# Hybrid encoder layer on one core: v quadrants and gate/up units loaded in the out projection pass, all w_out splits kept on chip, first down splits placed later

## The reference

```
u = _rmsnorm(h, norm1_g);  z = u @ w_in
a = gb * _short_conv(gc * xa, conv_w);  p = _multiscale_pool(xp, ...);  f = _fourier(xf)
mix = concatenate([_rms(a), _rms(p), _rms(f)]) * mix_g
h = h + mix @ w_out
v = _rmsnorm(h, norm2_g)
gu = v @ w_gate_up;  gate, up = gu[..., :D_FF], gu[..., D_FF:]
return h + (silu(gate) * up) @ w_down        # then a last RMSNorm
```

## Time and profile before

| what | value |
|---|---|
| median of 3 runs | 2538.41 us (2533.21 to 2539.73) |
| profiled execution: its time | 2538.45 us |
| its span | 2536.9 us |
| PE / DVE / ACT / POOL busy | 95% / 61% / 36% / 14% |
| PE idle ahead of the first gate/up matmul | 17.1 us |
| PE's granted clock, 870 to 886 us, 886 to 940 us | 0.55, 0.88 |
| the same, 940 to 1240 us | 1.00 |

### The profile page before, as it was taken

One profiled execution on the slowest core, in us unless ns is written; L12 is line 12 of the kernel. 1 busy time (PEld: TensorE's weight loads), 2 busy tenths in 40 slices (PEclk: granted clock), 3 DMA queues, 4 the chain that ended last, 5 costly groups with the idle time before them and its releaser, 6 DMA issues. The chain is left out here.

```text
span 2536.9 us, 32588 instructions
## 1 busy us (share of the span) xinstructions
PE 2411.9 (95%) x11786; PEld 2152.6 (85%) x11786; DVE 1547.4 (61%) x2312; ACT 902.9 (36%) x1486; POOL 360.1 (14%) x509
## 2 busy tenths in 40 slices
PE   6999999788999689999999999999999999999997
PEld 4887888677888589999999999899999788888886
DVE  4444545555878475565865556855556575686775
ACT  4121211142343343333433333433333333444543
POOL 0110110006444001111011111111111000100101
PEclk9999999887999899999999999999999999999999
DMA  5656872265566456667577765555554776687874
GB/s 184 212 132 167 215 200 61 92 201 199 195 253 216 154 185 206 213 215 199 185 224 221 220 199 163 162 180 177 181 171 142 251 237 189 211 304 222 268 231 138
DMA packets 216058, 492.95 MB, mean 194 GB/s; under 512 B 27552, under 2 KB 60866, under 8 KB 207469
## 3 DMA queue, kind: packets, MB, share of 16 engines
q1 hardware_dynamic: 188301, 358.99, 43.3%
q0 software_dynamic: 27616, 132.11, 17.5%
HBM read 395.90 MB, written 164.31 MB: 221 GB/s over the span
## 5 line engine op out<-in xcount | busy, mean ns | idle before, releaser
L81 PE MATMUL gu_bank<-v_form_hi_sb,gu_hi_sb 128*128 128x428 f32 (+1 forms) x1848 | 663.1, 359 | 38.1 <-DVE gu_lo_sb L1811 17.1
L82 PE MATMUL gu_bank<-v_form_lo_sb,gu_hi_sb 128*128 128x428 f32 (+1 forms) x1848 | 661.0, 358 | 0.0
L83 PE MATMUL gu_bank<-v_form_hi_sb,gu_lo_sb 128*128 128x428 f32 (+1 forms) x1848 | 660.6, 357 | 0.0
L1716 ACT ACTIVATE gu_hi_sb<-gu_raw_sb 128x512 fp32r<-128x512 f32 x462 | 285.9, 628 | 360.0 <-PE gu_bank L83 360.0
L1811 DVE TENSOR_TENSOR gu_lo_sb<-gu_raw_sb,gu_hi_sb 128x512 fp32r<-128x512 f32 x462 | 311.1, 686 | 157.8 <-ACT gu_hi_sb L1716 157.8
L81 PEld LDWEIGHTS gu_bank<-v_form_hi_sb,gu_hi_sb 128*128 128x128 f32 x1848 | 349.5, 189 | 57.5 <-issue 23.3
L83 PEld LDWEIGHTS gu_bank<-v_form_hi_sb,gu_lo_sb 128*128 128x128 f32 x1848 | 349.7, 189 | 11.3
L82 PEld LDWEIGHTS gu_bank<-v_form_lo_sb,gu_hi_sb 128*128 128x128 f32 x1848 | 349.8, 189 | 11.0
L82 PE MATMUL gu_bank<-gu_lo_sb,act_hi_sb 128*128 128x512 f32 x770 | 303.4, 394 | 0.0
L81 PE MATMUL gu_bank<-gu_hi_sb,act_hi_sb 128*128 128x512 f32 x770 | 301.8, 392 | 0.0
L83 PE MATMUL gu_bank<-gu_hi_sb,act_lo_sb 128*128 128x512 f32 x770 | 298.8, 388 | 0.0
(11 more groups left out here) (190 smaller groups left out, 3295.1 us busy)
## 6 DMA issues: line engine op xcount, KB each, us to landing
gu_raw_sb<-gu_sums SPq DMA_DIRECT2D x264, 256.0 KB, 3.9
gu_raw_sb<-w_gu_q SPq DMA_DIRECT2D x198, 256.0 KB, 2.7
gu_sums<-w_gu_q POOLq DMA_DIRECT2D x24, 1408.0 KB, 14.2
gu_raw_sb<-down_sums SPq DMA_DIRECT2D x132, 256.0 KB, 3.6
act_raw_sb<-act_forms SPq DMA_DIRECT2D x154, 192.0 KB, 3.7
gu_raw_sb<-w_down_q SPq DMA_DIRECT2D x99, 256.0 KB, 3.3
w_raw_sb<-w_panels SPq DMA_DIRECT2D x40, 512.0 KB, 3.5
act_raw_sb<-act_forms SPq DMA_DIRECT2D x77, 256.0 KB, 4.1
```

Source lines behind the costliest of these rows:

```text
L81: pe.matmul(out, w[0], x[0], start=first, stop=False, skip_group_check=True)
L82: pe.matmul(out, w[0], x[1], start=False, stop=False, skip_group_check=True)
L83: return pe.matmul(out, w[1], x[0], start=False, stop=last, skip_group_check=True)
L1716: act.activation(w_hi[:, s, :], raw[:, s, :], ACT.Copy).then_inc(w_hi_made, 1)
```

## The change

It has three parts.

1. `outproj` keeps all eight split panels of w_out on chip (`w_rest_hi`, `w_rest_lo` beside the four of `Feed`). The 32 loads and 64 split instructions of the blocks after the first go, and with them the places of these in the queues of SP, ACT and DVE. The room comes from sharing: the buffer of the gate/up units (`unit_raw`) also holds the mix input and the scratch of `outproj` and data of `fourier`, and v transposed is written over `w_raw`.
2. A new class `Seam` holds buffers and semaphores that live across the barrier. SP loads the quadrants A11 and A12 of the first pair in block 3, and the first six gate/up units in block 4, ahead of that block's h1 stores. The last block's vT store is cut in four, one per 128 tokens, and nothing waits for it before the barrier; ACT waits for it ahead of `read_out(0)`, SP ahead of unit 14. A22 and A21 are the first DMAs of `swiglu`.
3. At the end of gate/up the first six down activation splits are taken out of the last iteration: ACT has them all behind its last `read_out`, DVE has two ahead of the last `right_half` and four behind `act_sums`. The weight parts keep their places.

```diff
+class Seam:
+    def __init__(self, nc, ctx, c, gu):
...
+        self.raw = ctx.enter_context(nc.sbuf_tensor("unit_raw_sb", [P, UNIT_RING, UNIT], F32))
+        self.v_first = ctx.enter_context(nc.sbuf_tensor("v_first_sb", [P, 2, 4, max(HALVES)], F32))
...
+        self.loaded = KD - 2
+        self.vt_all = 16 * (NBLK - 1 + NT)
...
@@ outproj @@
-        vt = sb("v_turned", [P, KD, T])
-        mx2 = sb("mix_raw2", [P, KD - 2, T])
+        w_hi2, w_lo2 = (sb(n, [P, KD - RING, D], F32R) for n in ("w_rest_hi", "w_rest_lo"))
...
+        mx2 = seam.raw[:, 0:KD - 2, :]
+        vt = feed.w_raw.rearrange("p s (a n) -> p (s a) n", n=T)
...
+            def first_units():
+
+                sp.wait_ge(m_lo_made, KD * NBLK + 2)
+                sp.wait_ge(sq_made, SQUARES * (NBLK - 1))
+                gu.all_made(sp)
+                for u in range(KD - 2):
+                    sp.dma_start(mx2[:, u, :], seam.weights(u)).then_inc(seam.w_landed[u], 16)
...
-                for q in (0, 1):
-                    panel(KD * b + KD + q)
...
                 if b:
                     vt_store(b - 1)
+                if b == 3:
+                    sp.wait_ge(vt_stored, 32)
+                    first_v_load(A11)
+                    first_v_load(A12)
+                if b == NBLK - 1:
+                    first_units()
...
-            vt_store(NBLK - 1)
-            sp.wait_ge(vt_stored, 16 * NBLK)
+            for t in range(NT):
+                sp.wait_ge(vt_made, 8 * (NBLK - 1) + 2 * t + 2)
+                at = token(NBLK - 1) + P * t
+                sp.dma_start(c["vT"][:, at:at + P].rearrange("(k p) n -> p k n", p=P), vt[:, :, P * t:P * t + P])\
+                    .then_inc(vt_stored, 16)
             sp.wait_ge(h_stored, 16 * NT * NBLK)
...
-                    if KD * b + q + RING < PANELS:
-                        feed.split_panel_lo(dve, KD * b + q + RING)
+                    if b == 0 and q < KD - RING:
+                        dve.wait_ge(feed.w_hi_made, RING + q + 1)
+                        dve.tensor_tensor(w_lo2[:, q, :], feed.w_raw[:, q, :], w_hi2[:, q, :].bitcast(F32), ALU.subtract)\
+                            .then_inc(feed.w_lo_made, 1)
...
@@ swiglu @@
-            v_load(0, A11)
-            gu.all_made(sp)
+            v_load(0, A22)
+            v_load(0, A21)
             for u in range(GU_UNITS):
                 if u >= SLOTS:
                     sp.wait_ge(w_lo_made, u - SLOTS + 1)
-                sp.dma_start(raw[:, u % SLOTS, :], gu_weights(u)).then_inc(w_landed[u % SLOTS], 16)
+                if u >= seam.loaded:
+                    sp.dma_start(raw[:, u % SLOTS, :], gu_weights(u)).then_inc(w_landed[u % SLOTS], 16)
...
                 if f == 0:
                     act.wait_ge(used, u + 1)
+                    if u == 0:
+                        act.wait_ge(vt_stored, seam.vt_all)
...
             def w_split(u):
                 if u >= GU_UNITS:
-                    splits(u - GU_UNITS)
+                    if u % 2 == 0:
+                        down_w_split(u - GU_UNITS)
                     return
...
+            for u in range(AHEAD):
+                a_split(u)
             for u in range(ALL):
...
+            a_split(0)
+            a_split(1)
             right_half(ITER - 1, 1)
             act_sums(ITER - 1)
+            for u in range(2, AHEAD):
+                a_split(u)
```

More of the change, by code:

```diff
@@ L54 @@
 START = (0, 1, 2, 3)
-PANELS = NBLK * KD
 HF = MF // 2
@@ L1193, in token, with panel @@
             return SEQ - T * b
+        def panel(k):
+            first = k < RING
+            return [w[:, k - (0 if first else RING), :] for w in
+                    ((feed.w_hi, feed.w_lo) if first else (w_hi2, w_lo2))]
         def raw(b, k):
@@ L1471, in row_ranges, with swiglu @@
     return out
-def swiglu(nc, c, gu, dn, half, eps):
+def swiglu(nc, c, gu, dn, seam, half, eps):
     HM, SLOTS, AHEAD = max(HALVES), UNIT_RING, 6
@@ L1484, in swiglu @@
     ALL = UNITS * len(PAIRS)
-    A11, A21, A22, A12, AX = range(5)
     E_, N6, D_, S3 = range(1, 5)
@@ L1618, in v_load @@
                 n = HALVES[k]
[L1619 to L1621 removed]
+                row, at = v_source(k, where)
+                sp.dma_start(v_part(where, n), c["vT"][row:row + 512, at:at + n]
+                             .rearrange("(k p) n -> p k n", p=P)).then_inc(v_landed[where - 1], 16)
             def h_load(k, n):
@@ L1765, in splits @@
                     return
-                if u % 2 == 0:
+                if u % 2 == 0 and u >= AHEAD:
                     down_w_split(u)
```

174 lines of the change are left out of this document (99 added, 75 removed).

## The result

The changed kernel takes 2522.13 us (median of 5 runs, 2520.26 to 2525.1), the kernel before on the same chip 2539.73; the ratio is 0.9936, with a 95% interval of 0.9921 to 0.995. That is 17.6 us less where 27.6 were forecast. The profiled execution of the changed kernel took 2525.1 us, with a span of 2523.3; it is the longest of the five, so the profiles show a smaller gain (13.5 us of span) than the medians.

What follows compares the result with a forecast made beforehand. PE was taken as the bound, busy 2411.9 of 2536.9 us, so only its waits and lower clock could be won: 5.2 + 16.7 + 5.7 = 27.6 us off 2538.4 gave 2511 us, with 2503 to 2521 holding 8 in 10.

Steps and rivals of the forecast that it cites:

- Part 1: Out projection: without panel splits ahead of the adds, PE's three waits for them, 5.2 us in all, go.
- the bound that I had given: Out projection: gain between 0 and 5.2 us, since no more idle than that stands there.
- Part 2: Seam between out projection and gate/up: early loads start unit 3 15.8 us earlier, plus 0.9 for the clock: 16.7 us.
- 0.9 as half of 1.8: Seam, unit 3: a 3.3 us wait might or might not lower the clock; half of the possible 1.8 us gain taken.
- A: Rival at the seam: slow vT quarters make A22 late; 2525.5 us, or 2515 to 2519 in a milder form; chance 0.13.
- D: Rival at the seam: vT store so slow that `read_out(0)` holds PE; slower than before, about 2542 us; chance 0.04.
- Part 3: End of gate/up: the 6.0 us wait goes, a 2.6 us wait ahead of the first down matmul appears; gain 5.7 us.
- Idle of 2.6 us left the clock up: Start of the down stage: clock stays up behind the new wait, as behind 2.89 us; a fall would cost 1.8 us.
- The other stalls ... and the tail are not touched: The other 6.9 us of L1877 stalls, the stalls ahead of 594 us and the tail were claimed to stay untouched.
- where nothing but the places of buffers changes: Ahead of 594 us only buffer places change; a growth there was named as a sign of being wrong.
- The strong form of A: Seam: four vT quarters of 5.3 us each, one behind the other; seam gives only 1 to 3 us; 2525.5 us; chance 0.06.
- C: Rival: little gain in the out projection and a lower clock at the end of gate/up; 2518 us; chance 0.13.

Runs made afterwards that it cites:

- the put-back load: Changed kernel with DVE work (32 four-piece subtractions) put back in the out projection where the kernel before split a panel: 2540.32 us.
- the 128 bytes: Changed kernel with 128 bytes more per partition ahead of the v forms, shifting the down stage's activations against its weights: 2507.26 us.
- the early splits: On top of the 128 bytes, DVE makes the low parts of the first two down activations ahead of its last two gate/up readings: 2503.24 us.
- the last kernel: Changed kernel with the 128 bytes, the early splits, v form rows 1792 bytes apart and the w_rest buffers 192 bytes further on: 2506.53 us.

## Why the prediction was wrong

**Part 1, forecast 5.2 us: the waits went.** None of the three stalls at the adds is left, and the last group of transposes begins 260.3 us after the stage's start instead of 266.3, though the w_rest products take 1.1 us more. These 6.0 us lie 0.8 above the bound that I had given; where that comes from no row shows. By trial only the direction is shown (the put-back load).

**Part 2, forecast 16.7 us: the waits came where I had put them, but the part gave about 1.9 us less.** With part 1, unit 3 was to start 21.0 us earlier. It starts 18.6 earlier by the trace and 20.2 earlier counted from the start of the out projection, 0.8 short; 6.0 of the 20.2 were won ahead of the last transposes, so 14.2 are left for the 15.8 of the seam. Step by step: the block ends 1.5 us later than it would have, since SP's issue of the last vT quarter took 1.84 us where I had taken 0.37; PE 4.3 us behind ACT's first split (4.3 forecast); units 0 and 1 in 6.9 us (7.5); A22 late for ACT by 1.3 (0.8); a wait of 0.4 us ahead of unit 2 (none); 3.8 us ahead of unit 3 (3.3). The clock did not stay up behind these 3.8 us. It fell 0.9 us into unit 3 and cost 1.7 us, for 2.2 before: 0.6 won, where I had taken 0.9 as half of 1.8. The four vT quarters took 4.8 us each in the median from issue to landing, overlapping, and the last had landed 9.4 us behind the first one's issue, so rivals A and D fell. The run without early loads gives them 13.2 us of the whole.

**Part 3, forecast 5.7 us: the wait and its successor came as put down**, 6.0 us gone and 2.49 there for a forecast 2.6. "Idle of 2.6 us left the clock up" does not hold in general: here the clock fell a microsecond after the down stage's start and cost 1.6 us, where I had named 1.8. Of the nine profiles with this wait ahead of the down stage five show the fall and four don't; the five are all of those with the distance 128, the four have 0, 64, 160 and 192. Whether that is chance no run shows. Undoing the part costs 5.0 us.

**The step that failed** is the one that closed the first paragraph, "The other stalls ... and the tail are not touched", and with it the silent term of the sum: that the 770 products of the down stage go on at their pace. In my list of what could refute me I wrote of places of buffers as if they were nothing ("where nothing but the places of buffers changes"), and looked for their effect only ahead of 594 us. The change had moved the weights by 30080 bytes and the activations by -17856, from 192 to 128 modulo 256, and that is 10.3 us. For the profiled pair the sum then reads 27.0 - 1.65 (start) - 1.6 (clock) - 10.3 = 13.5 us. The second profile of the changed kernel, with 0.697 us per product and an earlier start, gives 27.1 - 0.35 - 1.6 - 8.0 = 17.1 us, near the 17.6 of the medians. Of the rivals none held this. The strong form of A, 2525.5, and C, 2518, lay nearest to the 2522.13; A's reason, quarters that end one far behind the other, did not come, and of C's only the lower clock did.

My range ended at 2521 since all its bounds came from waits, and PE's own pace had none. The trace of before did hold a hint: its out projection took 0.680 us for the product for which its down stage took 0.687, with the same 128x512 shape, full clock and no idle. I had the two durations and did not ask why they differ.

The version with the change, the 128 bytes and the early splits beats both kernels, with 2503.24 us: 35 us under before (0.9865 of it) and 19 under the changed kernel.

## What to carry to other kernels

When an edit moves buffers, treat the pace of every matmul stage as a term of its own: compare the matmuls' durations per shape between stages of the kernel before, and list where the operands lie before and after. A padding line of 64 to 192 bytes is a cheap experiment, and here 128 bytes gave 14.9 us, more than parts 1 and 3 of the change together. When a wait is taken away, ask what the waiting engine's next need is and what stands ahead of it in the queue: the 2.5 us at the down stage went by moving the first two low parts ahead of DVE's last readings.

## What the runs showed that I had not expected

- The pace of 128x512 matmuls that stand at the full clock with no idle depends on where the operands lie: 0.680, 0.687 or 0.700 us for three of them, 3% from end to end, and all sixteen profiles sort by the distance of their buffers modulo 256 bytes alone. For the 424 to 428 columns of gate/up the rule gave nothing.
- At one distance the same program showed 0.697 in one execution and 0.700 in another, each constant over 540 us.
- A wait can cost clock after it seems to be over. Ahead of unit 3, behind 3.0 to 4.2 us of idle that began at the full clock, eleven of twelve profiles go on at the full clock and fall 0.3 to 1.3 us later, for nine or ten matmuls 0.36 us apart (some 1.7 us); one, the last kernel's with 3.39 us, does not fall. At the down stage, behind the same 2.49 us, five of nine fall within 1.6 us and four don't. The length of a wait alone does not tell.
- Four dependent DVE subtractions of 256 columns took 1.78 us in one place and 5.29 in another of the same block; GpSimd's squares ran beside the slow ones and not beside the fast ones.
- One DMA issue on SP took 1.84 us, behind three like it of 0.37 us, and held the end of the block.
